# Delta rule on Trainium2: products on half of TensorE's array widened to the whole array

## What is computed

```
c = DN_CHUNK                         # 64
u, w = sol[..., :dv], sol[..., dv:]  # from the triangular solve of each chunk
q_dec = q * jnp.exp(g)[..., None]
k_dec = k * jnp.exp(g_last[..., None] - g)[..., None]

def chunk_step(state, inp):
    q_i, k_i, u_i, w_i, a_i, gl_i = inp
    v_new = u_i - jnp.einsum("bhcd,bhdv->bhcv", w_i, state)
    o_i = jnp.einsum("bhcd,bhdv->bhcv", q_i, state) + jnp.einsum("bhij,bhjv->bhiv", a_i, v_new)
    state = state * jnp.exp(gl_i)[..., None, None] + jnp.einsum("bhcd,bhcv->bhdv", k_i, v_new)
    return state, o_i
```

## Time and profile before

| What | Value |
|---|---|
| Median of 3 runs | 2415.54 us (2415.13 to 2416.78) |
| Profiled execution, span (the page gives no other time for it) | 2418.1 us |
| TensorE matmul busy | 2341.3 us (97%) |
| TensorE weight load busy | 2132.2 us (88%) |
| VectorE, ScalarE, GpSimd busy | 1125.0, 1113.8, 1706.9 us |
| DMA | 149 GB/s mean over the span |

### The profile page before, as it was taken

The page is one execution under the profiler, slowest core; times in us unless marked ns, Lnnn a source line. Parts: engine busy times, 40 slices in busy tenths (PEclk is TensorE's granted clock), DMA queues, the critical chain, the costliest instruction groups (busy, mean ns, idle before and its releaser), DMA issues.

```text
span 2418.1 us, 40330 instructions
## 1 busy us (share of the span) xinstructions
PE 2341.3 (97%) x15689; PEld 2132.2 (88%) x15689; DVE 1125.0 (47%) x1947; ACT 1113.8 (46%) x1273; POOL 1706.9 (71%) x1340
## 2 busy tenths in 40 slices
PE   8999899999999999999999999999999999999998
PEld 7888889999988888898899999889898888898887
DVE  3334755432333333365664142333524666433776
ACT  4335444447443443454444654335555335555433
POOL 6998545546799899974455568997545997645996
PEclk9999999999999999999999999999999999999999
DMA  7555323224455555552233344655333555423553
GB/s 240 191 191 164 116 88 105 89 88 141 158 191 190 191 175 191 191 157 88 88 99 102 100 150 162 200 187 172 123 101 115 191 191 169 137 88 124 189 191 131
DMA packets 312357, 359.97 MB, mean 149 GB/s; under 512 B 18660, under 2 KB 291104, under 8 KB 312096
## 3 DMA queue, kind: packets, MB, share of 16 engines
q1 hardware_dynamic: 311866, 357.75, 45.6%
q10 hardware_dynamic: 358, 0.33, 0.0%
HBM read 357.01 MB, written 1.05 MB: 148 GB/s over the span
## 4 chain that ended last, share of the span: by engine, by line
PE 85%; DVE 10%; ACT 2%; issue 1%; POOL 1%; DMA 0%; SPq 0%; DVEq 0%; ACTq 0%
PE ps L751 21%; PE ps L551 21%; PE ps L583 16%; PE ps L588 9%; PE ps L630 3%; PE ps L837 1%; PE ps L790 1%; PE ps L646 1%; PE ps L844 1%; POOL sb_lo L524 1%; DVE sb_kT L1864 1%; PE ps L1125 1%; DVE sb_vT L1864 1%; PE ps L846 1%; PE ps L617 1%
## 5 line engine op out<-in xcount | busy, mean ns | idle before, releaser
L524 POOL TENSOR_TENSOR sb_lo<-sb_raw,sb_hi 128x512 fp32r<-128x512 f32 (+1 forms) x1336 | 1706.7, 1313 | 693.3 <-ACT sb_hi L1226 692.9
L1226 ACT ACTIVATE sb_hi<-sb_raw 128x2048 fp32r<-128x2048 f32 (+3 forms) x341 | 639.1, 1876 | 658.5 <-PE ps L588 349.2
L583 PE MATMUL ps<-sb_hT,sb_hi 128*128 128x512 f32 x1792 | 426.1, 390 | 0.0
L583 PEld LDWEIGHTS ps<-sb_hT,sb_hi 128*128 128x128 f32 x1792 | 332.9, 188 | 66.5
L751 PE MATMUL ps<-sb_hT,sb_hi 128*128 128x256 f32 x2304 | 312.4, 288 | 5.0 <-DVE sb_hT L1993 2.8
L751 PEld LDWEIGHTS ps<-sb_hT,sb_hi 128*128 128x128 f32 x2304 | 286.6, 192 | 11.0 <-DVE sb_hT L1993 3.2
L588 PEld LDWEIGHTS ps<-sb_hT,sb_lo 128*128 128x128 f32 x1792 | 229.8, 191 | 8.7
L1784 DVE TENSOR_TENSOR sb_yinv<-ps,sb_row 128x512 f32<-128x512 f32 x112 | 77.5, 692 | 335.3 <-PE ps L588 335.2
L588 PE MATMUL ps<-sb_hT,sb_lo 128*128 128x256 f32 x1792 | 232.5, 283 | 0.0
L551 PE MATMUL ps<-sb_hi,sb_o_h 128*128 128x512 f32 x560 | 219.8, 393 | 0.9 <-DVE sb_o_l L1791 0.9
L551 PE MATMUL ps<-sb_hi,sb_o_l 128*128 128x512 f32 x560 | 218.8, 391 | 0.0
(11 more groups left out here) (379 smaller groups left out, 3665.2 us busy)
## 6 DMA issues: line engine op xcount, KB each, us to landing
sb_raw<-in_ffn_w_in SPq DMA_DIRECT2D x88, 1024.0 KB, 5.1
sb_raw<-in_w_in SPq DMA_DIRECT2D x78, 1024.0 KB, 5.2
sb_raw<-in_ffn_w_out SPq DMA_DIRECT2D x44, 1024.0 KB, 4.9
sb_raw<-in_ffn_w_up SPq DMA_DIRECT2D x44, 1024.0 KB, 5.1
sb_raw<-in_ffn_w_down SPq DMA_DIRECT2D x22, 1024.0 KB, 4.9
sb_raw<-in_w_out SPq DMA_DIRECT2D x16, 1024.0 KB, 5.1
sb_raw<-in_w_branch_a SPq DMA_DIRECT2D x8, 1024.0 KB, 5.1
sb_raw<-in_w_branch_b SPq DMA_DIRECT2D x8, 1024.0 KB, 5.1
```

The source lines that it names most:

```text
L524: ins = nc.gpsimd.tensor_tensor(lo[:, slot, c], raw[:, slot, c], hi[:, slot, c].bitcast(F32), ALU.subtract)
L583: mm(ps[:, bank + i, :].rearrange("p (h n) -> p h n", h=2), wh[:, c, i * P:(i + 1) * P], hT_both[:, :, c, :], start=c == 0, stop=False, sk ...
L1226: fn(hi[:, slot, 0:width], raw[:, slot, 0:width], ACT.Copy).then_inc(hi_ready, 1)
```

## The change

All products of the three kinds become products of 128 rows and 128 columns. The row products take whole blocks of `o_h` and `o_l` and a selector of 128 rows that is zero outside the eight and eight rows. The correction multiplies all 128 columns of `w_k`; VectorE still reads only the 64 result rows of the chunk. A push multiplies all 128 rows: for a first chunk the keys come from `k_dec`, whose lower half (rows 64 to 127) is now always zero, for a second chunk from a new place `k_late` (the tile `row`, free during the mixer), whose upper half is zero. So VectorE writes the keys in two pieces of 64 rows, and the second piece only where a second chunk is pushed (problems 0 and 2). It also clears `select` and the lower half of `k_dec` at the start, and the upper half of `k_late` once a layer.

```diff
-        select = sb("select", [ROW_LOW + HEADS, HEADS], F32R)
+        select = sb("select", [P, HEADS], F32R)
...
-        row_parts = tuple(o[0:ROW_LOW + HEADS, k, :] for o, k in ((o_h, 6), (o_h, 7), (o_l, 6)))
+        row_blocks = tuple(o[:, k, :] for o, k in ((o_h, 6), (o_h, 7), (o_l, 6)))
+        row_parts = tuple(o[0:ROW_LOW + HEADS, :] for o in row_blocks)
+        k_late = row
...
-                for n, row in enumerate(row_parts):
+                for n, row in enumerate(row_blocks):
...
-                        ins = mm(ps[:, 4 + n, i * S:(i + 1) * S], select[:, h:h + 1].to_broadcast([ROW_LOW + HEADS, P]), row, start=True, stop=True)
+                        ins = mm(ps[:, 4 + n, i * S:(i + 1) * S], select[:, h:h + 1].to_broadcast([P, P]), row, start=True, stop=True)
...
                 def push(ch):
                     t, half = divmod(ch, 2)
-                    rr = slice(64 * half, 64 * half + 64)
                     for i in range(2):
                         p = 2 * i + t
-                        ins = mm(ps[:, 4, i * P:(i + 1) * P], of(k_dec, p)[rr, :], of(u_v, p)[rr, :], start=True, stop=True)
+                        keys = of(k_late, i) if half else of(k_dec, p)
+                        ins = mm(ps[:, 4, i * P:(i + 1) * P], keys, of(u_v, p), start=True, stop=True)
...
-                        ins = mm(ps[rr, 5, i * P:(i + 1) * P], of(w_k, 2 * i + t)[:, rr], state[:, ch - 1, i, :], start=True, stop=True)
+                        ins = mm(ps[:, 5, i * P:(i + 1) * P], of(w_k, 2 * i + t), state[:, ch - 1, i, :], start=True, stop=True)
...
-                        ts(of(k_dec, i), ps[:, 7, i * P:(i + 1) * P], col(3, i), None, ALU.mult)
+                        first, late = slice(0, CHUNK), slice(CHUNK, P)
+                        ts(of(k_dec, i)[first, :], ps[first, 7, i * P:(i + 1) * P], col(3, i)[first, :], None, ALU.mult)
+                        if i % 2 == 0:
+                            ts(of(k_late, i // 2)[late, :], ps[late, 7, i * P:(i + 1) * P], col(3, i)[late, :], None, ALU.mult)
...
+                V.memset(k_late[0:CHUNK, :], 0.0)
                 dve.wait_ge(start_loaded, 16)
...
-            own.link(V.tensor_copy(select[:, :], ident[0:ROW_LOW + HEADS, 0:HEADS]))
+            own.link(V.memset(select[:, :].bitcast(F32), 0.0))
+            own.link(V.tensor_copy(select[0:ROW_LOW + HEADS, :], ident[0:ROW_LOW + HEADS, 0:HEADS]))
             own.link(V.tensor_copy(select[ROW_LOW:ROW_LOW + HEADS, :], ident[ROW_LOW:ROW_LOW + HEADS, ROW_LOW:ROW_LOW + HEADS]))
+            V.memset(k_dec[CHUNK:P, :], 0.0)
```

More of the change, by code:

```diff
@@ L867, in delta @@
                 for ch in range(1, 4):
-                    t, half = divmod(ch, 2)
-                    rr = slice(64 * half, 64 * half + 64)
+                    t = ch // 2
                     if ch == 3:
```

## The result

| | Before | Changed |
|---|---|---|
| Median, 4 runs each | 2416.16 us (2415.13 to 2417.57) | 2403.85 us (2400.9 to 2405.9) |
| Profiled execution, span | 2418.1 us | 2401.7 us |
| TensorE matmul busy | 2341.3 us | 2319.8 us |
| VectorE busy | 1125.0 us | 1133.3 us |

The ratio is 0.9946 (95% interval 0.9934 to 0.9958): 12.3 us faster. The forecast was 18.2 us faster, 2397.3 us; the time lies inside the range, the direction is right, and the gain is a third smaller than forecast.

A forecast was written before the change was run, and what follows sets the result against it. TensorE was taken as the bound. Switches removed, 19.8 us, less 1.6 for VectorE's additions gave 18.2 off: span 2418.1 to 2399.9, and 2397.3 us with the runs' median 2.6 below the span; range 2392.5 to 2406.

The forecast's parts named there:

- The switches: Delta stage on TensorE: each switch between full and partial array costs about 0.19 us (0.13 entering 64 columns); removing them saves 19.8.
- The wider load: Corrections on TensorE load 128 columns, 0.192 in place of 0.137 us, 96 times; taken as 0, 5.3 us if bare.
- Rival 2: Corrections on TensorE: the wider weight load is bare and costs 5.3 us, giving 2402.6 us; chance 0.06.
- Rival 1: Behind pushes and corrections: TensorE's next waits swallow all 42 saved exits, 8.0 us less gain, giving 2405.3 us; chance 0.10.
- Rival 3: Partial products: the 0.19 us belongs to their operands and stays, 2422.4 us, chance 0.04; with the load hidden 2417.1, chance 0.04.
- 3 x 2 layers x 0.26 = 1.6 us: VectorE's added scalings in levels 0 and 2 delay TensorE at three level waits a layer, 0.26 us each, 1.6 in all.
- rows don't shorten it (I assume): VectorE's added 64x128 scaling takes 0.26 us back to back; fewer rows were assumed not to shorten it.
- The other ten are covered: The remaining ten of 16 added VectorE scalings hide behind unit products or VectorE's own wait; uncovered they cost 2.6 us more.
- With all steps shifted each may come or go: Five clock falls (280, 1079, 1785, 1833, 2116 us), 1.5 us each, may each come or go; two allowed either way, 3 us.
- The base: Profiled span 2418.1 us less 18.2 gives 2399.9; the runs' median lies 2.6 below that span, so 2397.3 was predicted.
- TensorE's summed idle otherwise as before: Sign to check: apart from the level wait growing from 13.0 to about 14.6 us, TensorE's total idle stays unchanged.

The follow-up runs named there:

- f3: Changed kernel with the two second-chunk key scalings moved from levels 0 and 2 to level 4, beside f1 on one chip: 2397.97 us, ratio 0.9919.
- e4: Kernel before with the corrections alone on the whole array (128 columns of w_k in place of 64), nothing added on VectorE: 2410.27 us, ratio 0.9964.
- e2: Kernel before with the row products alone on the whole array, only a clearing added on VectorE: 2412.28 us, ratio 0.9969.
- e6: Changed kernel with the second key scaling over all 128 rows in place of rows 64 to 127, executed once: 2395.64 us.
- e9: Changed kernel, unaltered, run again beside other experiments on one chip: 2404.12 us, ratio 0.995 against the kernel before.
- f1: Changed kernel, unaltered, run again as the base of four combinations on one chip: 2404.21 us, ratio 0.9947 against the kernel before.
- f4: Changed kernel with the second scalings in level 4 and 16 unread transposes filling TensorE's first-pair wait in both layers: 2396.13 us, ratio 0.9912.
- e1: Changed kernel with the two second-chunk key scalings moved from levels 0 and 2 to level 4, on another chip than f3: 2398.44 us, ratio 0.9917.
- e7: Kernel before with VectorE's additions alone (keys in two pieces, clearings), TensorE's products still partial: 2419.58 us, ratio 1.0015.

## Why the prediction was right in direction and too large

**The switches: right.** 19.8 us were to go, that is 9.5 a layer up to the fourth pair's last correction, and 0.3 behind it. The stage of f3 is 261.93 - 252.15 = 9.8 shorter, with waits 0.5 longer, of which the first pair's row products' 0.6 were told ahead. Gross 10.3, less the 0.6: 9.7. The three parts alone agree within 0.2 each. The Trainium skill (TensorEngine Tiling (Array Packing), Key Properties) says that changing the tiling mode drains TensorE. These runs agree, with 0.19 us a switch.

**The wider load: right**, at nothing behind work. Rival 2 (2402.6) comes close to the measured time and is still wrong: e4 excludes its mechanism. A number that fits is no evidence of a cause.

**Rival 1, exits given back: wrong.** f3 keeps every exit and is 19.4 us faster. **Rival 3, the switch isn't the shape: wrong** by the first piece of the chain, 0.45.

**The step that failed is "3 x 2 layers x 0.26 = 1.6 us" for VectorE.** Two things were wrong in it.
- The size. The prediction took the duration of the full-height scaling for one on rows 64 to 127, "rows don't shorten it (I assume)". They don't: the 64-row L1938 takes 330 to 335 ns in all 32 cases. But the piece behind it takes 0.36, not 0.26, and lengthens its successor by 0.09. Each delayed level paid 0.47 to 0.49, at all three levels that the prediction names.
- The count. "The other ten are covered" missed the third pair. There TensorE waits for the unit evacuation behind level 0 (0.29 before, 1.07 after, at 410.14) and for the level behind it (0.55 before, 1.02 after, at 418.40). The prediction read the level waits, and not the short wait for L1864 that is late next. The two waits, before and then after:

```profile
413.35 1.70 PE L751 MATMUL ps<-sb_hT,sb_hi 128*128 128x256 f32 x12 [0.29 <-DVE sb_qT L1864]
421.14 1.13 PE L837 MATMUL ps<-sb_levels 128*128 128x128 f32 x8 [0.55 <-DVE sb_levels L1942]
...
410.14 1.69 PE L753 MATMUL ps<-sb_hT,sb_hi 128*128 128x256 f32 x12 [1.07 <-DVE sb_qT L1865]
418.40 1.13 PE L839 MATMUL ps<-sb_levels 128*128 128x128 f32 x8 [1.02 <-DVE sb_levels L1946]
```

Together the additions lengthen the waits by 1.4 (first pair: 0.48 and 0.47; second: 0.49) and 1.3 (third pair) a layer, 2.7 and not 0.8; the wait behind the Gram products gave 0.8 of it back, so that 1.9 a layer, 3.8 us in all, stand where 1.6 was forecast.

The part of it in the second pair has a trace of its own. VectorE's masking of the levels ahead of the inverse, before and then after, in the second pair:

```profile
334.68 1.30 DVE L1921 TENSOR_TENSOR sb_levels<-sb_levels,sb_const 128x512 f32<-128x512 f32 x1
```

```profile
332.89 0.86 DVE L1922 TENSOR_TENSOR sb_levels<-sb_levels,sb_const 128x512 f32<-128x512 f32 x1
```

The same instruction, 0.44 shorter, and TensorE's wait is shorter by 0.42. GpSimd's split of a unit starts 1.8 us ahead of it in the kernel before (332.88) and 1.0 ahead in the changed one (331.91). Its length ranges from 0.93 to 1.86 before and from 0.69 to 1.42 after. In all 24 cases of three kernels (before, changed, e2) it ends 1.8, 3.1 or 4.3 us behind the start of GpSimd's splits, whenever it began, in steps of about one split (1.27 us at 338.67 in the changed kernel). That fits a masking held up by a split; no run varied GpSimd by itself, so the cause isn't shown.

**The clock was left symmetric.** "With all steps shifted each may come or go" treats a fall as chance. This one hangs on the very wait that the change lengthens: at 2.75 us it came every time. The fall at 1079 that it stands in for cost nothing. The second layer's new fall costs 1.5 us, and it belonged into the sum as soon as the term of 0.26 stood at this wait.

**The base was a long execution of its kernel, on two of three chips.** The profiled execution's span was 2418.1, and a device time is 1.8 us more than its span in the kernel before, so its time was some 2419.9, against the 2415.13 to 2417.57 of the others. Of fifteen executions of the kernel before that ran beside e6 to e9 the spans are 2412.8 (mean granted clock 0.998) to 2416.2 (0.996), of eleven beside f1 to f4 2412.9 to 2418.7, mean 2415.3; thirteen beside e1 to e4, on a third chip, have 2415.5 to 2420.9. The profiled one had three falls behind 1780 us, at 1785, 1833 and 2117, and the changed kernel's has two, at 1817 and 2100.

The account: 18.2 forecast; less 2.2 for VectorE's waits (3.8 in place of 1.6); less 1.5 for the new fall; that leaves 14.5. One fall fewer in the rest of the program makes it 16.0, and the two profiled spans differ by 16.4. The medians differ by 12.3. Of the 2.2 between that and 14.5, 0.4 lies outside the span: a device time is 2.2 us more than its span in the changed kernel, where it is 1.8 before. On the chip of f1 the mean spans differ by 13.6 (2415.3 and 2401.7). The rest, 1 to 2 us, I put down to the falls of before, whose usual execution has fewer than the profiled one. That part isn't shown, since no second profile of it was taken.

Of the marks that were to show it: pushes at 0.45, twelve behind at 1.43 (1.44), corrections 0.45 and row products 0.46 are as told. The second pair, from its row products (326.30 and 325.23) to the next pair's (394.19 and 390.94), is 2.18 shorter, forecast 2.3; here 0.42 of gift hides that VectorE took more. The wait at the levels is 16.8, not 14.6, and "TensorE's summed idle otherwise as before" fails at three lines of the ledger.

## What to carry to other kernels

A product of part of the array among full ones costs some 0.19 us on entry (0.13 into 64 columns) and again on exit, and saves TensorE nothing in return, since zeros in the unused rows or columns cost it nothing; so widen it, and pay for the zeros on an engine and in a step that nothing waits for. When work is added to an engine that is waited for, follow it to every wait behind it, the small ones too, and put it where its result is needed last. And price a wait of TensorE's such as the 2.75 us here together with the clock behind it: sixteen idle products in each of two such waits gave 3.1 us by the stages and 3.7 by the medians, nearly what the pushes save in a layer.

## What the runs showed of the hardware that was not expected

- VectorE, between neighbours on rows 0 to 127 and 0 to 63, takes 0.36 us for a scaling on rows 64 to 127 and 0.49 for the next one, and 0.26 and 0.40 if the same scaling covers all rows: doing twice the work is 0.19 us faster.
- A wait of 2.75 us ahead of the level products brought a fall of the granted clock in 10 of 10, one of 2.27 in 3 of 10 (all in the first layer), and a filled one in 0 of 6; each fall in a stage cost 1.5 us, and one at 1079, ahead of a wait for ScalarE, cost nothing.
- One and the same addition on VectorE cost 0.8 us of waits a layer in the kernel before (e7), and in the changed one 2.0 more than in level 4 (14.7 in f1, 12.7 in f3), through the waits that lay behind it.
